# Five 1024x1024 projections of a mixer computed with seven block products in place of eight

## What is computed

```python
def mixer_block(u, cos, sin, w_in, conv_w, q_norm_g, k_norm_g, w_conv_out, w_attn_out, w_o):
    proj = u @ w_in
    cb, cc, cx, q, k, v, gc, ga = split_columns(proj)
    z = depthwise_conv_centred(cc * cx, conv_w)
    y_conv = (cb * z) @ w_conv_out
    q = rmsnorm(q.reshape(B, S, N_HEADS, HEAD_DIM_2), q_norm_g)
    k = rmsnorm(k.reshape(B, S, N_KV_HEADS_2, HEAD_DIM_2), k_norm_g)
    v = v.reshape(B, S, N_KV_HEADS_2, HEAD_DIM_2)
    q = apply_rope(q, cos, sin) * (HEAD_DIM_2 ** -0.5)
    k = apply_rope(k, cos, sin)
    y_attn = bidirectional_gqa(q, k, v) @ w_attn_out
    merged = jax.nn.sigmoid(gc) * y_conv + jax.nn.sigmoid(ga) * y_attn
    return merged @ w_o
```

## Time and profile before

| | us |
|---|---|
| median of 3 runs | 1967.65 (1965.8 to 1970.3) |
| span of the profiled execution, first to last instruction | 1961.2 |
| five projections and attention on TensorE | 534.58 to 693.13 |
| `yc` and `ya` | 693.13 to 748.65 |
| experts, first gather to the last | 785.8 to about 1690 |

### The profile page before, as it was taken

One profiled execution on the slowest core, in us unless ns is written; L12 is line 12 of the kernel. 1 busy time (PEld: TensorE's weight loads), 2 busy tenths in 40 slices (PEclk: granted clock), 3 DMA queues, 4 the chain that ended last, 5 costly groups with the idle time before them and its releaser, 6 DMA issues.

```text
span 1961.2 us, 20936 instructions
## 1 busy us (share of the span) xinstructions
PE 1610.4 (82%) x9098; PEld 966.8 (49%) x9098; DVE 604.4 (31%) x1395; ACT 294.3 (15%) x793; POOL 11.6 (1%) x35
## 2 busy tenths in 40 slices
PE   9999999999999999866556666555666566899999
PEld 7775567755688886322222222212222212457886
DVE  3673455634242412411201111101111101145533
ACT  1243313432112001100000000000000000223220
POOL 0000000000000000000000000000000000000000
PEclk9999999999999999987788887788887778999999
DMA  9761276423443463899999999999999999944200
GB/s 367 252 159 51 99 267 214 130 89 119 169 148 129 177 252 149 349 430 434 428 433 430 430 431 430 432 429 432 429 430 430 432 431 429 371 153 172 92 38 22
DMA packets 92869, 553.34 MB, mean 282 GB/s; under 512 B 4480, under 2 KB 11392, under 8 KB 79968
## 3 DMA queue, kind: packets, MB, share of 16 engines
q1 hardware_dynamic: 91920, 548.81, 69.9%
q0 software_dynamic: 848, 3.05, 0.4%
HBM read 550.80 MB, written 1.05 MB: 281 GB/s over the span
## 4 chain that ended last, share of the span: by engine, by line
PE 62%; DMA 34%; DVE 2%; ACT 1%; issue 0%; SPq 0%; POOL 0%; ACTq 0%; DVEq 0%; POOLq 0%
PE bank L664 29%; DMA ring<-in_w 21%; DMA arena<-in_w 12%; PE bank L1129 8%; PE bank L691 6%; PE bank L673 6%; PE bank L1157 3%; PE bank L652 3%; PE bank L1447 1%; PE bank L873 1%; PE bank L805 1%; PE bank L785 1%; DMA prm<-in_pk 0%; DVE arena L2098 0%; PE bank L1400 0%; PE bank L1100 0%
## 5 line engine op out<-in xcount | busy, mean ns | idle before, releaser
L664 PE MATMUL bank<-arena,ring 128*128 128x256 f32 x1856 | 412.2, 380 | 1.0 <-DVE arena L2356 0.5
L1129 PE MATMUL bank<-ring,arena 128*32 128x512 f32 x1216 | 288.0, 732 | 150.3 <-DMA arena<-in_w 98.6
L664 PEld LDWEIGHTS bank<-arena,ring 128*128 128x128 f32 x1856 | 348.9, 190 | 50.9 <-issue 4.3
L1129 PE MATMUL bank<-arena 128*32 128x512 f32 x832 | 234.8, 736 | 100.8 <-DMA ring<-in_w 100.8
L1129 PEld LDWEIGHTS bank<-ring,arena 128*32 128x32 f32 x1216 | 72.2, 132 | 272.3 <-issue 272.3
L664 PE MATMUL bank<-ring,arena 128*128 128x512 f32 (+3 forms) x520 | 205.1, 544 | 1.0 <-DVE arena L2468 1.0
L1129 PEld LDWEIGHTS bank<-arena 128*32 128x32 f32 x832 | 57.2, 132 | 187.4 <-issue 187.2
L1157 PE MATMUL bank<-ring,arena 128*32 128x512 f32 x576 | 118.8, 659 | 24.1 <-DMA arena<-in_w 13.4
L664 PEld LDWEIGHTS bank<-ring,arena 128*128 128x128 f32 x520 | 96.2, 190 | 83.4 <-issue 71.3
L691 PE MATMUL bank<-ring,arena 128*128 128x512 f32 (+1 forms) x320 | 127.4, 555 | 1.3 <-DVE arena L1970 0.5
L673 PE MATMUL bank<-arena,ring 128*64 128x256 f32 x1024 | 112.7, 380 | 0.0
(11 more groups left out here) (394 smaller groups left out, 1414.5 us busy)
## 6 DMA issues: line engine op xcount, KB each, us to landing
ring<-in_w SPq DMA_DIRECT2D x53, 4096.0 KB, 31.6
arena<-in_w SPq DMA_DIRECT2D x35, 4096.0 KB, 37.1
ring<-in_w_in SPq DMA_DIRECT2D x40, 2048.0 KB, 7.9
ring<-in_w_ada SPq DMA_DIRECT2D x6, 2048.0 KB, 13.5
ring<-in_w_out SPq DMA_DIRECT2D x6, 2048.0 KB, 8.2
arena<-in_w SPq DMA_DIRECT2D x6, 2048.0 KB, 11.9
ring<-in_w SPq DMA_DIRECT2D x6, 2048.0 KB, 8.4
ring<-in_w_out SPq DMA_DIRECT2D x16, 512.0 KB, 10.7
```

The source lines that it names most:

```text
L664: i = te.matmul(ps, lhsT, rhs, start=n0 + k == 0, stop=n0 + k == n - 1)
L1129: m = te.matmul(ps[32 * j:32 * j + 32, :], LM.xg[:, f, 128 * k + 32 * j:128 * k + 32 * j + 32], vs[j][:, 512 * (k % 2):512 * (k % 2) + 512 ...
```

## The change

Each projection's weights are cut into four 512x512 blocks (two halves of the contraction, chunks 0 to 3 and 4 to 7, by two halves of the columns, ring entries 0 and 1) and the activations into four of 512x128 (the same halves of the contraction, by two halves of the tokens). Winograd's form of Strassen's algorithm makes the product from 7 block products in place of 8, with four sums of weight blocks (`weight_sum`, each 128x2048 elements), four of token blocks made once (`token_sums`, each 128x512), and seven sums of results (`to_sum`, `part_sum`, each 128x512 out of a bank). Every block product (`times`) is 16 matmuls with 128 moving columns, in a bank of its own (banks 0 to 3 in turn; the attention has 4 to 7). Five projections so have 35 products of 16 matmuls, 560, where they had 320 of 256 columns.

```diff
 def mixer_order():
-    for _ in range(48):
+    for i in range(7 * len(SEVEN) + 8):
         out.append("conv")
-        if n < MIX_ATT:
+        if i >= 2 and n < MIX_ATT:
             out.append("att")
+SEVEN = ("cc", "gc", "ga", "cx", "cb")
...
+            sums = [ar(14352 + 512 * k, 4, 128) for k in range(4)]
+            t1, t2 = (ring[:, 4, 2048 * k:2048 * k + 2048].rearrange("p (c n) -> p c n", n=512) for k in range(2))
+            t4 = ring[:, 5, 0:2048].rearrange("p (c n) -> p c n", n=512)
...
-                        for w in at.all(("att2", "PE"), ("att2", "DVE"), ("att2", "ACT")):
+                        for w in at.all(("att2", "PE"), ("att2", "DVE"), ("att2", "ACT"), ("mm", "P", "cb", 7)):
                             s.wait_ge(*w)
...
+            def times(group, w, xT, b):
+                ps = fresh(*group, b=b)
+                for i in range(4):
+                    m = product(ps[:, 128 * i:128 * i + 128], [(w[:, c, 128 * i:128 * i + 128], xT[:, c, :]) for c in range(4)])
+                m.then_inc(*t.done("mm", *group))
+            def seven_products(name, n, xT, sums):
+                times(("P", name, 1), w0[:, 0:4, :], xT[:, 0:4, lo], 7 * n % 4)
+                yield
+                times(("P", name, 2), w0[:, 4:8, :], xT[:, 4:8, lo], (7 * n + 1) % 4)
+                yield
+                ready(("T", name, 2), ("S", 3))
+                times(("P", name, 3), L2.t2, sums[1], (7 * n + 2) % 4)
...
             def mixer_branches():
-                ready(*[("ev", "cb", ch) for ch in range(8)])
+                for n, name in enumerate(SEVEN):
+                    yield from seven_products(name, n, L2.uT, L2.sums)
+                ready(*[("sum", "cb", part) for part in (11, 22, 12)])
...
+            def weight_sum(name, k):
+                ready(("w", (name, 0)), ("w", (name, 1)))
+                if k == 1:
+                    ready(("mm", "P", old, 4) if old else ("used", ("os", 1, 1)))
+                    ve.tensor_tensor(L2.t1, w1[:, 0:4, :], w0[:, 0:4, :], ALU.subtract).then_inc(*v.done("T", name, 1))
+                if k == 2:
+                    ve.tensor_tensor(L2.t2, w1[:, 4:8, :], L2.t1, ALU.subtract).then_inc(*v.done("T", name, 2))
...
             def mixer_branches():
+                for n, name in enumerate(SEVEN):
+                    weight_sum(name, 4)
+                    if name == "cb":
+                        tap(2)
+                    yield
+                    if name == "cb":
+                        tap(2)
+                    yield
+                    to_sum(L2.s2, name, 3, L2.s1, ("ev", "P", name, 1))
+                    part_sum(name, 11, 2, L2.s1)
+                    if name == "cb":
+                        tap(2)
+                    yield
+                    to_sum(L2.y1, name, 4, L2.s2)
+                    if new:
+                        weight_sum(new, 1)
+                    if name == "cb":
+                        tap(2)
+                    yield
+                    to_sum(L2.s3, name, 5, L2.s2)
+                    part_sum(name, 22, 4, L2.s3, L2.s2)
+                    if new:
+                        weight_sum(new, 2)
+                    yield
+                    part_sum(name, 12, 6, L2.y1)
+                    if new:
+                        weight_sum(new, 3)
+                    yield
+                    part_sum(name, 21, 7, L2.s3)
+                    yield
...
                     out_copy(("v2", tt), L2.vt[:, tt, :], bank("v2", tt)[:, 0:256])
+                    if tt == 0:
+                        weight_sum("cc", 1)
+                        weight_sum("cc", 2)
+                    else:
+                        token_sums(L2.uT, L2.sums)
+                        weight_sum("cc", 3)
```

More of the change, by code:

```diff
@@ L446, in sync_program, with load @@
             turn = [5]
-            def load(name, *srcs, width=512, kc=8):
-                i = turn[0] % NR
-                turn[0] += 1
+            def load(name, *srcs, width=512, kc=8, slot=None):
+                i = turn[0] % NR if slot is None else slot
+                turn[0] += slot is None
                 slot_of[name] = i
                 v = weights(name, width, kc)
-                for w in at.all(*([("used", users[i])] if users[i] else [])):
+                for w in at.all(*([("used", users[i])] if users[i] else []),
+                                *([("used", users[i], "sums")] if users[i] and users[i][0] in SEVEN and users[i][1] == 0
+                                  else [])):
                     s.wait_ge(*w)
@@ L914, in mixer_branches @@
                 ready(*every)
[L915 to L922, removed]
-                ready(*[("ev", "cb", ch) for ch in range(8)])
+                for n, name in enumerate(SEVEN):
+                    yield from seven_products(name, n, L2.uT, L2.sums)
+                t.also("used", ("T",))
+                ready(*[("sum", "cb", part) for part in (11, 22, 12)])
                 for g in range(2):
@@ L926, in mixer_branches @@
                     for i in range(4):
-                        feat(("yc", 4 * g + i), L2.zT, weights(("yc", g)), 128 * i)
+                        if g + i == 0:
+                            ps = fresh("yc", 0)
+                            product(ps[:, 0:256], [(weights(("yc", 0))[:, c, 0:128], L2.zT[:, c, :]) for c in range(4, 8)], 0, 8)
+                            ready(("sum", "cb", 21))
+                            product(ps[:, 0:256], [(weights(("yc", 0))[:, c, 0:128], L2.zT[:, c, :]) for c in range(4)], 4, 8
+                                    ).then_inc(*t.done("mm", "yc", 0))
+                        else:
+                            feat(("yc", 4 * g + i), L2.zT, weights(("yc", g)), 128 * i)
                         if i == 3:
@@ L1661, in mixer_branches @@
             def mixer_branches():
[L1662 to L1665, removed]
-                    yield
[L1667 to L1671, removed]
+                a.wait_ge(*at.of("z0"))
+                for n, name in enumerate(SEVEN):
+                    old = SEVEN[n - 1] if n else None
+                    ready(("mm", "P", name, 1), *([("sum", old, 11)] if old else []))
+                    se.copy(L2.s1, heads(bank("P", name, 1)[:, :], 128)).then_inc(*a.done("ev", "P", name, 1))
+                    yield
+                    if old in ("gc", "ga"):
+                        dst = L2.gcT if old == "gc" else L2.gaT
+                        ready(*[("sum", old, part) for part in (11, 12, 21, 22)])
+                        se.activation(dst, dst, ACT.Tanh, scale=0.5).then_inc(*a.done("gate", old))
+                    for _ in range(6):
                         yield
-                for _ in range(24):
+                for _ in range(8):
                     yield
@@ L2346, in mixer_branches @@
[L2346 to L2354, removed]
-                    ready(("mm", "cb", ch), ("z", ch))
-                    ve.tensor_tensor(zz, zz, bank("cb", ch)[:, 0:256], ALU.mult).then_inc(*v.done("ev", "cb", ch))
-                    yield
```

120 lines of the change are left out of this document (97 added, 23 removed).

## The result

The changed kernel takes 1970.77 us (median of 9 runs, 1969.30 to 1973.61), the kernel before 1966.35 (9 runs) beside it: ratio 1.0024, 95% interval 1.0016 to 1.0033. It is 4.4 us slower; the forecast was 5.2, with "slower" the likeliest. An eighth fewer multiplications bought nothing.

The account below looks back on a forecast made before the run. It took TensorE to bound the mixer, with VectorE having 100 us idle. Terms -13.3 - 0.5 + 4.6 + 8.9 + 1.5 + 4.0 = +5.2 us gave a span of 1966.4, time about 1973; range 1965 to 1979.

Parts of the forecast that it names:

- Products: On TensorE in the projections, 35 products of 3.57 us replace 40 chunks of 3.45 us, saving 13.3 us.
- the 0.5 of `yc`: Before `yc`, the 0.5 us wait for `cb`'s last copy is covered, since `yc` begins with the ready half.
- Prices on VectorE: On VectorE, a result sum costs 0.72 us and a weight sum 2.32 us, gaps included.
- Wait A: At the head, the second tile's first chunk on TensorE comes 4.6 us late, behind two weight sums on VectorE.
- Wait B: At the transposes, TensorE waits 8.9 us for rotated q and k behind VectorE's 37.0 us; some 2 one product earlier.
- Wait C: In `cb`, TensorE waits 1.5 us for VectorE, up to the copy of the second probabilities.
- Clock: Behind the waits at the head and the transposes, TensorE's clock falls to half, costing 1.7 and 2.3, 4.0 us in all.
- Rival 1: The waits in the mixer come but the clock stays: +1.2 us, 1969; chance 0.30.
- Moved transfers: The experts' first two weight tiles and `w_o`, loaded after `cb`'s last product, fit there and cost nothing.
- The base: For the whole kernel, the profiled execution's span of 1961.2 us, with the median 6.4 us above the span.
- Rivals 2 to 4: In the mixer: weight sums of 1.6 us, 0.06; products of 3.84, +11.7 us, 0.13; loads binding at 190 ns, +80, 0.02.

Follow-up runs that it names:

- after: The changed kernel as first measured and traced, beside the kernel before: 1970.77 us, ratio 1.0024.
- e3: Changed kernel with each weight sum working on 64 of its 512 columns, TensorE's work unchanged: 1952.25 us, ratio 0.9936 to the kernel before.
- e10: e5 with the attention one product later on TensorE and ScalarE alone, VectorE's order kept: 1951.74 us, ratio 0.9935 to the kernel before.
- e1: Changed kernel with the first two weight sums moved ahead of the copy of the first tile's v: 1961.97 us, ratio 0.9987 to the kernel before.
- e6: Changed kernel with 3 and 5 unused 512-column matmuls on TensorE in the two long waits: 1966.01 us, ratio 1.0006 to the kernel before.
- e9: e5 with the attention one product later still on all engines: 1957.03 us, ratio 0.9961 to the kernel before.
- e0: The changed kernel itself, measured again beside later runs: 1969.18 us, ratio 1.0025 to the kernel before.
- e8: Changed kernel with the first weight sum of `cx`, behind the rotation, made twice: 1969.38 us, ratio 1.0027 to the kernel before.
- e2: Changed kernel with 5 and 7 unused 512-column matmuls on TensorE in the two long waits: 1967.89 us, ratio 1.0017 to the kernel before.
- e7: Changed kernel with the first weight sum of `gc`, in the chain to the rotation, made twice: 1970.74 us, ratio 1.0031 to the kernel before.
- e5: Changed kernel with the edits of e1 and e4 together: 1956.29 us, ratio 0.9961 to the kernel before.
- e4: Changed kernel, VectorE doing two attention steps before the first result sums, attention one product later on all engines: 1963.87 us, ratio 0.9999 to the kernel before.

## Why the prediction was right, step by step

- **Products**, -13.3: right. Ten products are the row 542.49 of after, 35.89 with the tail of the last; one lasts 3.57 (606.99 to 610.56). 35 of them are 125.0 us, so -13.2, and e3 and e10 give 13.7 and 13.6 with the 0.5 of `yc` (e10: 12.2, and lost are 0.3 in a gap ahead of the transposes, 0.7 in the wait in `cb` and 0.4 in the work behind it). Instructions of 128 columns from 542.49 to 578.1, by shape (columns as in the earlier trace rows):

```profile
L675 PE MATMUL bank<-arena,ring 128*128 128x128 f32 x319 | 35.8, 275 | 0.0
L675 PEld LDWEIGHTS bank<-arena,ring 128*128 128x128 f32 x319 | 35.7, 192 | 0.0
```

A weight load's record still lasts 192 ns, but one is finished every 0.112 us: loads overlap one another, as the gather had shown. By the rule of the Trainium skill's page "TensorE: Matmul & The Clock Gate", section "Part 3: Packing small matmuls" (a load overlaps a running matmul only in other row groups), this stretch could not be as short: its 320 loads of 0.192 us would take 61 us one after another. The same page's "Step-by-step: what each phase is for" also allows a load to be pulled ahead into a background weight buffer. With that the length of the stretch agrees; the buffer itself no trace shows.

- **Prices on VectorE**: a weight sum takes 2.28 to 2.29, where the line through 512 and 1280 elements gave 2.29. The Trainium skill, page "VectorE: DVE Perf Modes", section "The TRN2 errata — SBUF-src ops pay a fixed extra latency per instruction", gives for such an addition (N + 151) / 0.96 ns, 2291 for 2048 elements; the trace agrees at 2284 ns.
- **Wait A**, +4.6: 4.43, and e1 shows that only the two sums make it.
- **Wait B**, +8.9: 1.90 + 6.39, or 8.73 from the end of eleven products (542.49 + 11 x 3.573) to the transposes. The chain of 37.0 us was 37.0. Both parts came where they were put: the "some 2" ahead of the fourth product of `gc`, the rest at the transposes.
- **Wait C**, +1.5: 1.21.
- **Clock**, +4.0 (A 1.7, B 2.3): 1.71 and 2.64 by e6 against after. B is the term that was a little short. That it came so near is partly luck: behind the waits at the transposes the traces show anything from 1.4 to 2.9 (last section), and the lengths in the sum were taken from two waits of the experts. Rival 1, that the clock stays, falls.
- **Moved transfers** and the experts, 0: right, by the rows (no wait for a transfer in the mixer) and by the table.
- The sum of the measured terms: -13.2 - 0.5 + 4.4 + 8.7 + 1.2 + 4.35 = +5.0, against 5.15 of the mixer, 4.4 to 4.8 of the medians.
- **The base**: here a step failed, without effect on the difference. I took the device time as 6.4 us above the span ("The median lies 6.4 above the span"). In the kernel after the profiled execution took 1973.61 at a span of 1971.9, 1.7 us outside the span. The execution profiled before was thus one of the faster ones, not 6.4 short of its time. Such an offset should not have been read off two different executions. The 6.4 is the first median less that span, so adding the two gives the median back, and the forecast of 1973 is 1967.65 plus 5.2; of the 2 us by which it is above 1970.77, 1.3 are that first median (1966.35 over 9 runs) and 0.8 the difference.
- **Rivals 2 to 4** (cheap weight sums, 3.84 a product, loads that bind) are excluded by the rows above.

## What to carry to other kernels

Work moved from a saturated engine to one with spare time costs mainly by where it stands in that engine's queue, not by its sum: VectorE had 36 us to spare in the stretch of the projections and still made TensorE wait 9.5 us at three places in it, and 4.4 ahead of it, while a few lines of reordering turned +0.24% into -0.65%. When two in-order engines share a list of steps, look for the long dependent chain between them and give the waiting engine more to do ahead of it (e10), not both (e9). Price a wait of a few microseconds on TensorE together with the slow stretch behind it, and separate the two by unused matmuls that end inside the wait.

## What the runs showed of the hardware that I had not expected

The clock falls behind rather short waits, and not reliably. Over all traces of the mixer: waits of up to 1.22 us were never followed by a granted clock of 0.50; one of 1.9 (1.89 or 1.90) was in two traces (e0, e8) and was not in four (after, e1, e2, e6), at the same place with the same work before it; all of 3.1 us and more were (3.11 to 6.39). I had priced it from waits of 4.48 and 5.95 and put no fall at 1.9. The product behind the wait of 1.9, in after and then in e0 (columns as in the earlier trace rows):

```profile
580.28:583.95 3.67, 3.67 (x32) 3.65 (x32) 3.63 (x2) 0.00 (x0) 0.00 (x0) 1.00 0.09 12
```

```profile
578.44:583.91 5.47, 5.47 (x32) 5.27 (x32) 5.37 (x5) 0.00 (x0) 0.00 (x0) 0.69 0.38 110
```

What decides it at 1.9 is open; no run was made for it.

What a fall costs is the part of it that lies on work. After e0's wait of 4.75 us the stretch up to the scores took 15.30, in e7 14.53, in e5 14.33, in e4 15.85 and in after 15.60, with the same work each time and 12.96 at full clock. So such a wait costs 1.4 to 2.9 us more. e4 and e5 had the same length of wait (3.70 and 3.68) and stand near the two ends, so its length doesn't decide which; what does, no run here shows.
